# A hybrid decoder step on one core: three attention stages joined into one program, and weight casts moved from ScalarE to GpSimd

## What is computed

```
xn = rmsnorm(x) ; h = xn @ w_in                # 1024 -> fq fk fv ff fz | hq hf hi hz | mq mz | ga gb gm
A  = forgetting attention over fq, fk, fv      # 8 heads x 64, causal, plus sums of log gates
B  = gated linear recurrence (HGRN2)           # 4 heads, state 128x128, chunked
M  = attention into 256 memory tokens          # 4 heads x 128, keys and values mk, mv from mem @ w_mk, w_mv
y  = rmsnorm(x + (sig(ga)*(A*silu(fz))@w_pa + sig(gb)*(norm(B)*silu(hz))@w_pb + sig(gm)*(M*silu(mz))@w_pm) @ w_o)
```

## Time and profile before

| | us |
|---|---|
| median of 3 runs (3035.96 to 3053.45) | 3039.75 |
| the profiled execution | 3042.43 |
| its span, first to last instruction | 3040.4 |
| TensorE busy in the span | 2802.5 (92%) |
| VectorE busy | 1577.6 (52%) |
| ScalarE busy | 1098.7 (36%) |
| GpSimd busy | 728.0 (24%) |
| mean granted TensorE clock | 0.967 |

### The profile page before, as it was taken

The page is one execution under the profiler, slowest core; times in us unless marked ns, Lnnn a source line. Parts: engine busy times, 40 slices in busy tenths (PEclk is TensorE's granted clock), DMA queues, the critical chain, the costliest instruction groups (busy, mean ns, idle before and its releaser), DMA issues. The chain is left out here.

```text
span 3040.4 us, 38617 instructions
## 1 busy us (share of the span) xinstructions
PE 2802.5 (92%) x13880; PEld 2295.6 (76%) x13880; DVE 1577.6 (52%) x3007; ACT 1098.7 (36%) x2086; POOL 728.0 (24%) x743
## 2 busy tenths in 40 slices
PE   7889988899998889898789998999999978999998
PEld 5668767677776778687678877888888866888887
DVE  5414578433341467665345555656664546444544
ACT  1212111333332345443245554555554223232322
POOL 6027655123223343433020061011020014000000
PEclk9999989899998999999999999999999989999999
DMA  5576678756653656565745564555444546333331
GB/s 167 222 237 202 210 222 262 239 155 186 194 166 129 217 198 232 188 213 183 234 140 163 160 187 140 163 158 154 142 140 130 198 174 194 124 110 115 116 109 49
DMA packets 290765, 526.33 MB, mean 173 GB/s; under 512 B 110270, under 2 KB 135423, under 8 KB 269327
## 3 DMA queue, kind: packets, MB, share of 16 engines
q1 hardware_dynamic: 237519, 403.41, 42.2%
q0 software_dynamic: 17440, 55.98, 6.5%
q10 hardware_dynamic: 35616, 64.47, 5.6%
HBM read 411.09 MB, written 112.68 MB: 172 GB/s over the span
## 5 line engine op out<-in xcount | busy, mean ns | idle before, releaser
L2528 PE MATMUL fill_out<-keep_hi,fill_x 128*128 128x512 f32 x2112 | 739.8, 413 | 87.4 <-DMA fill_x<-x_tiles 47.2
L2528 PEld LDWEIGHTS fill_out<-keep_hi,fill_x 128*128 128x128 f32 x2112 | 391.7, 193 | 160.8 <-issue 36.1
L2528 PE MATMUL fill_out<-keep_lo,fill_x 128*128 128x512 f32 x1056 | 433.8, 411 | 3.9 <-PEq L3215 3.9
L413 ACT ACTIVATE fox_pt_hi<-fox_turned 128x512 fp32r<-128x512 f32 (+1 forms) x320 | 170.1, 531 | 321.2 <-PE fox_turned L363 319.3
L466 DVE TENSOR_TENSOR fox_pt_lo<-fox_turned,fox_pt_hi 128x512 fp32r<-128x512 f32 (+1 forms) x320 | 194.9, 609 | 169.2 <-ACT fox_pt_hi L413 166.7
L452 DVE CUSTOM_DVE_ANT_0 fox_probs<-fox_scores,fox_bias 128x512 f32<-128x512 f32 (+2 forms) x320 | 187.6, 609 | 106.1 <-PE fox_scores L352 56.2
L2528 PEld LDWEIGHTS fill_out<-keep_lo,fill_x 128*128 128x128 f32 x1056 | 203.6, 193 | 35.7 <-issue 4.3
L2150 ACT ACTIVATE in_stage<-in_out 128x512 f32<-128x512 f32 (+1 forms) x119 | 70.4, 594 | 433.8 <-PE in_out L99 385.2
L2628 POOL CAST keep_hi<-fill_raw 128x512 fp32r<-128x512 f32 x48 | 30.2, 628 | 652.3 <-PE fill_out L2539 616.9
L363 PE MATMUL fox_turned<-ident,fox_probs 128*128 128x128 f32 x1088 | 173.2, 274 | 7.1 <-ACT fox_probs L404 6.4
L97 PE MATMUL mf_out<-mf_w_hi,mf_t_hi 128*128 128x512 f32 x408 | 166.7, 409 | 9.0 <-DVE mf_w_lo L3031 8.1
(11 more groups left out here) (382 smaller groups left out, 6391.2 us busy)
## 6 DMA issues: line engine op xcount, KB each, us to landing
fill_x<-x_tiles SPq DMA_DIRECT2D x132, 1024.0 KB, 5.4
dc_slot<-in_cache_fox_k_dram SPq DMA_DIRECT2D x128, 256.0 KB, 3.9
dc_slot<-in_cache_fox_v_dram SPq DMA_DIRECT2D x128, 256.0 KB, 3.3
in_raw<-in_w_in_dram POOLq DMA_DIRECT2D x104, 256.0 KB, 3.6
plain<-fill_stage ACTq DMA_DIRECT2D x96, 256.0 KB, 5.5
mf_gate<-plain SPq DMA_DIRECT2D x96, 256.0 KB
turned<-in_stage ACTq DMA_DIRECT2D x64, 256.0 KB, 3.9
fill_raw<-in_w_in_dram POOLq DMA_DIRECT2D x56, 256.0 KB, 3.2
```

The source lines that it names most:

```text
L413: act.activation(pt_hi[:, zeta % PT_SLOTS, skip:BANK], bank_of(st)[:, skip:BANK], ACT.Copy).then_inc(hi_ready, 1)
L2528: ins = pe.matmul(self.out[n % self.OUTS][:], x, w, start=(k == 0 and term == 0), stop=(ends and term == 2))
```

## The change

The three stages become one Block in one `cleanup_on_exit`; what stood at a stage's start is issued near the end of the one before, and waits stand where one stage's tiles lie over another's. The recurrence's tail of 4 slots is gone; of its 96 fill matmuls 16 go to the prompt attention's first slots (two of 24, four of 12, four of 16) and 80 to its key slots. ScalarE's casts go to GpSimd in project_and_decode and in the recurrence. In the first seven passes slice k is split k ticks into the pass. The diff, without changes of indentation and cut to its core:

```diff
-    steps = [("fill", 0)] + [("queries", 0, b) for b in range(QUADS)] + [("values", 0, b) for b in range(QUADS)]
+    steps = [("open", 0), ("fill", 0), ("open", 1), ("fill", 1), ("open", 2)] + [("queries", 0, b) for b in range(QUADS)]
     for b in range(QUADS):
-        steps += [("fill", 1 + b), ("keys", 0, b)]
+        steps += [("keys", 0, b), ("fill", 2 + b)]
+    steps += [("values", 0, b) for b in range(QUADS)]
...
+                    if st == ("open", 0):
+                        recur.computed(sp)
+                        fill.wait_stored(sp, needed)
+                        load_queries(sp, 0)
+                        for n in range(2):
+                            load_keys(sp, *quads[n])
+                    if st == ("open", 1):
+                        recur.store_state(sp)
+                        recur.store_rows(sp, 0)
+                        load_values(sp, 0)
+                        load_bias(sp, 0)
+                    if st == ("open", 2):
+                        recur.store_rows(sp, 1)
+                        for n in range(2):
+                            load_z(sp, *quads[n])
...
+        split_at = steps.index(("key", *quads[-1], QUADS))
...
+        def _(sp):
+            sync_steps(sp, steps[:split_at])
...
                     if kind == "keys":
+                        if n == 0:
+                            recur.computed(pe)
...
+                    if (h, i) == (0, 0):
+                        recur.all_stored(act)
                         act.wait_ge(most_ready, h * NT + i + 1)
...
                         if i == 0:
                             dve.wait_ge(bias_loaded, 16 * (h + 1))
+                    if (h, i) == (0, 0):
+                        recur.all_stored(dve)
...
+        def computed(eng):
+            eng.wait_ge(state_ready, len(chunks))
+            eng.wait_ge(o_taken, len(chunks))
...
-        fill.begin(fill.spread(matmuls, 2 * (len(chunks) + AHEAD)) + fill.spread(last_matmuls, TAIL), True)
+        fill.begin(fill.spread(matmuls, 2 * (len(chunks) + AHEAD)))
...
+            prompt.scores_done(sp)
+            fill.wait_stored(sp, needed)
+            sp.dma_start(k_rows[:], mem_k.rearrange("(t p) c -> p t c", p=P)).then_inc(kv_loaded, 16)
+            sp.dma_start(v[:], mem_v.rearrange("(t p) c -> p t c", p=P)).then_inc(kv_loaded, 16)
+            load_q(sp, 0)
+            load_z(sp, 0)
+            load_q(sp, 1)
+            paged.sync_start(sp)
+            prompt.sync_rest(sp)
...
+            prompt.all_stored(sp)
+            load_z(sp, 1)
...
                 fill.tensor(pe, 0)
+                prompt.banks_free(pe)
                 pe.wait_ge(kv_loaded, 32)
...
-            return (n - 1) * U + (k // 2 if n < G else k)
+            return (n - 1) * U + k
...
-                def low(m):
+                def split_slice(m):
                     hi, lo = w_ring.at(ring_at[m])
+                    pool.wait_ge(raw_loaded[m % RAWS], 16 * ((m - KT) // RAWS + 1))
+                    ring_free(pool, m)
+                    pool.tensor_copy(hi, raw[m % RAWS][:]).then_inc(cast, 1)
                     pool.wait_ge(cast, m - KT + 1)
                     pool.tensor_tensor(lo, raw[m % RAWS][:], hi.bitcast(F32), ALU.subtract).then_inc(split, 1)
...
-                def high(m):
-                    act.wait_ge(raw_loaded[m % RAWS], 16 * ((m - KT) // RAWS + 1))
-                    ring_free(act, m)
-                    act.activation(w_ring.at(ring_at[m])[0], raw[m % RAWS][:], ACT.Copy).then_inc(cast, 1)
...
-MATMULS = {"recur": 1340, "recur_last": 96, "fox_first": 144, "fox": 1472, "fox_last": [10, 12], "memory_first": 16}
+MATMULS = {"recur": 1340, "fox_first": [24, 24] + [12] * 4 + [16] * 4, "fox": 1552, "fox_last": [10, 12], "memory_first": 16}
...
-                with nc.cleanup_on_exit():
-                    recur_prompt(nc, core, turned[PT["hq"]], turned[PT["hf"]], plain[PN["hi"]][0:T, :],
+                with nc.cleanup_on_exit(), nc.Block() as block:
+                    recur = recur_prompt(nc, core, block, turned[PT["hq"]], turned[PT["hf"]], plain[PN["hi"]][0:T, :],
```

More of the change, by code:

```diff
@@ L4 @@
+from collections import namedtuple
 from contextlib import ExitStack
@@ L99, in product, with attend_prompt @@
     return pe.matmul(out, a[0], b[1], start=False, stop=last)
-def attend_prompt(nc, core, queries, fox_k, fox_v, z_fox, neg_c, gated, fill, matmuls, first_matmuls, last_matmuls):
+def attend_prompt(nc, core, block, queries, fox_k, fox_v, z_fox, neg_c, gated, fill, matmuls, first_matmuls, last_matmuls, recur, needed):
     QUADS = NT // 4
@@ L488, in recur_prompt, with rows, load_queries @@
-def recur_prompt(nc, core, queries, gates, values, z_hg, gain, gated, state_out, fill, matmuls, last_matmuls, needed):
+        def rows(dram, head, first, count):
+            return dram[first * P:(first + count) * P, head * FD:(head + 1) * FD].rearrange("(t p) c -> p t c", p=P)
+        def load_queries(sp, head):
+            if head >= 1:
+                sp.wait_ge(q_ready, head * QUADS)
+            for half in range(2):
+                sp.dma_start(q_raw[half * FD:(half + 1) * FD, :],
+                             rows_of(queries, head * FD, FD)).then_inc(q_loaded, 16)
@@ new lines, in load_values, with load_keys @@
+        def load_values(sp, head):
+            if head >= 1:
+                sp.wait_ge(v_ready, head * QUADS)
+            sp.dma_start(v_raw[:], rows(fox_v, head, 0, NT)).then_inc(v_loaded, 16)
+        def load_keys(sp, head, b):
+            n = head * QUADS + b
+            if n >= 2:
+                last = quads[n - 2]
+                sp.wait_ge(turned_ready, turn_at["keys", last[0], last[1]] + 1)
+            for half in range(2):
+                sp.dma_start(k_raw[n % 2][:, :, half * FD:(half + 1) * FD], rows(fox_k, head, 4 * b, 4)
+                             ).then_inc(k_loaded[n % 2], 16)
@@ L490, in recur_prompt @@
+        return AttentionEnd(lambda sp: sync_steps(sp, steps[split_at:]), scores_done, banks_free, all_stored)
+def recur_prompt(nc, core, block, queries, gates, values, z_hg, gain, gated, state_out, fill, matmuls):
     CH = 4
@@ L502, in recur_prompt, with walk @@
     BLOCK = HH * CH
-    PARTS, AHEAD, TAIL = 4, 5, 4
-    def walk(prepare, early, late, post, extra, tail):
+    PARTS, AHEAD = 4, 5
+    def walk(prepare, early, late, post, extra):
         for n in range(-AHEAD, len(chunks)):
@@ L897, in attend_memory @@
+        return RecurrenceEnd(computed, store_state, lambda sp, piece: store(sp, BLOCKS - 1, piece), all_stored)
+def attend_memory(nc, core, block, queries, mem_k, mem_v, z_mem, gated, last, fill, first_matmuls, needed, prompt):
     ST = NM // P
```

1332 lines of the change are left out of this document (644 added, 688 removed).

## The result

The changed kernel took 3025.45 us (median of five runs, 3020.97 to 3035.83), the kernel before 3041.46 beside it: a ratio of 0.9944, 95% interval 0.9925 to 0.9964. A second set of runs gave 3022.94 against 3044.99, ratio 0.9930 (0.9909 to 0.9952). So the change takes 16 to 22 us, 0.6 to 0.7%. I had predicted 3031, 8 us less than before. The run profiled here is the slowest of its five, 3035.83 (span 3034.1); the profile of the second set has 3020.5.

The account below looks back on a forecast made before the run. TensorE, busy 2802.5 of 3040.4 us, was taken as the bound, with at most 238 us of waiting to remove. 3042.43 - 8 - 8 + 5 + 3 = 3034.4 profiled, 3031.7 against the median, stated as 3031; range 3000 to 3048.

Parts of the forecast that it names:

- First joint: Recurrence to prompt attention: overhead of about 20 us falls to 12, so -8 us (-14 to -2).
- second joint: Joint to the memory attention: 8.1 us of TensorE idle and some lowered clock go, for -8 us (-11 to -3).
- The new wait: First joint: TensorE waits for a late x tile and an eviction behind ScalarE's root, 4.5 to 9.7 us, taken as 7.
- first score about 30 us after: Sign of being right: first score about 30 us after the last recurrence matmul, with 96 fill matmuls between.
- Casts in the recurrence: Moving casts to GpSimd there only renames TensorE's wait to `keep_lo`; idle time stays and +5 us come.
- The rival that ScalarE was the cause: Recurrence: ScalarE's evictions are the real limit and GpSimd's chain keeps up, giving about 2998 us; chance 0.18.
- Casts in project_and_decode: 104 casts moved to GpSimd there cost small waits at weight changes in the later passes: +3 us, from -10 to +15.
- one slice per tick in place of two evens the first passes out: First passes of project_and_decode: splitting one slice per tick evens out GpSimd's added cast work; no gain was priced.
- VectorE beside GpSimd: Project_and_decode: GpSimd's time can become VectorE's; 24 casts would at worst put 15 us on VectorE, where 3 is taken.
- the rival at 3057: GpSimd blocks VectorE in passes 1 to 7 of project_and_decode, costing 23 us, and the recurrence's 5 doubles; chance 0.11.
- Joints that close fully: Both joints: the first's x tile comes by 1459 and no clock falls, -20 and -9, giving 3019 us; chance 0.14.
- joints that don't: Both joints: SP's earlier loads delay the x tiles as long, only -2 and -3, giving 3043 us; chance 0.09.

Follow-up runs that it names:

- e1: Changed kernel with both cast moves undone (ScalarE casts, slices split as before), joined stages kept; 3030.62 us against 3044.31 for the kernel before.
- e8: Changed kernel with ScalarE casting everywhere, slice k still split k ticks into the first seven passes; 3027.20 us against 3044.50 for the kernel before.
- e2: Kernel before with the cast moves and the spread splits alone, three stages and barriers kept; 3039.76 us against 3044.31 for the kernel before.
- e4: Changed kernel with the x tile issued ahead of the prompt attention's queries and keys at the first joint; 3019.89 us against 3044.31 before.
- e6: Changed kernel with ScalarE casting again in the last seven passes of project_and_decode; 3016.29 us against 3044.99 for the kernel before.

## Why the prediction came out right, and which of its steps did not

The time was inside the range, and the chance for no change that can be told (0.47) stood just above that for faster (0.41), which is what came: 16 and 22 us, just past the 15 that I took as the least that can be told. The joints were worked out rightly. The casts were not, and the total came near partly by luck: two terms missed on the fast side (19 and 4.6 us) stand against two too small on the slow side (11 us together).

- **First joint, -8, and second joint, -8: right.** Column E of the pairs that differ in the joints alone gives -17 (e1 against before; e8, with the same joints, gives -11) and -15 to -18 (changed against e2). By place, in the first profiles: from the last recurrence matmul to the first score 63.0 became 37.6, of which 18.2 us (80 matmuls) only moved to the key slots, so **-7**. From the last `fox_turned` to the first `mem_turned` 11.7 became 8.5, and from there to the merge 135.6 became 130.1: **-9**. The new wait was forecast at 4.5 to 9.7, taken as 7: it is 6.54 and 6.55, and its two limits, SP's queue and ScalarE's root, both show in e4. The overhead is 13 for the 12 forecast. The sign "first score about 30 us after" was not that sum: 96 fill matmuls, 16 transposes and 12 us are 36, and 37.6 came. The x tile that I had late by up to 2.4 us behind the memory loads is late by 2.29.
- **Casts in the recurrence, +5: right in kind, short in size.** The waits changed name, at the places named and for the reasons named (the differences ahead of a slice, the two raw buffers). D says +9 over all profiles. I had also misread the list: the 18.0 us for low parts are of the whole span, and 6.8 of them, in four waits, are in the recurrence. The rival that ScalarE was the cause falls: it wanted a recurrence 20 us shorter, and the recurrence is longer.
- **Casts in project_and_decode, +3: wrong, and the reason why the sum came out too small.** The step that failed is "one slice per tick in place of two evens the first passes out", which I priced at nothing, with -10 as the bound. It is -19 (A). I had read ScalarE's wait for raw loads as the only thing the move could free. I had not read GpSimd's own list, where 60.6 us for ScalarE's casts stood in the first seven passes, some 37 of them ScalarE's order and not the ring, with the cache multiplies of the decoding rows behind it. That these waits are the cause is the likeliest reading of the four cells, and no run isolates it. Against that I had also missed a cost: the sample rows use all eight slices at a pass's start, and slice 7, split in the last tick behind the multiplies, is late by 1.3 to 7.5 us in five passes.
- **The last seven passes: the working was right at one change and wrong at five.** At the last change of weights I wrote 1.2 us, from a chain of 10.6 us against a margin of 9.4; it is 1.09:

```profile
924.36 0.50 PE L98 MATMUL in_out<-rest_hi,x_first 128*128 128x512 f32 x1 [1.09 <-POOL rest_lo L2110]
```

  For the five earlier ones I took 0.3 us each, trusting decode matmuls between. They are 1.25 to 1.93 us, six in all 9.0; B says +10, and e6 takes it back.
- **The stage's end, -4.6: not in the prediction at all.** It is TensorE's wait for the recurrence's first x tile, 14.8 us before and 10.1 after. See the last section.
- **VectorE beside GpSimd**: the rival at 3057 wanted TensorE's waits for VectorE up by 15 us and the first passes longer. From 152 to 575 us these waits fell from 42 us to 24 and 23, and the passes are shorter. VectorE's busy time over column A (the same 222 instructions), before and in the two changed profiles (us, PE, PEld, DVE, ACT, POOL, clock, DMA share, GB/s):

```profile
152.16:581.68 429.52, 381.45 (x1649) 300.36 (x1649) 230.50 (x222) 83.14 (x146) 226.58 (x168) 0.94 0.73 230
153.17:570.32 417.15, 374.55 (x1649) 295.82 (x1650) 227.92 (x222) 57.29 (x99) 283.83 (x228) 0.95 0.75 240
153.53:560.69 407.16, 375.25 (x1649) 295.99 (x1649) 220.40 (x222) 57.06 (x98) 286.40 (x228) 0.95 0.77 245
```

  It falls by 3 and 10 us while GpSimd's rises by 57 and 60. The Trainium skill's rule (Advanced Engine Details and Errata, VectorE Performance Modes) is that GpSimd instructions and VectorE's two-port ones block each other at the shared port; my prediction left out the two ports. No view shows which of its instructions were two-port ones. The added casts did not make VectorE busier here.
- **Joints that close fully, joints that don't, ScalarE as the cause**: the first is refused by the 8.9 us of waits still there, the second by E, the third by D.

By the runs, the sum of the step sizes is -16 (joints) + 9 (D) - 19 (A) + 10 (B) - 4.6 (C), about -21 for a change measured at -16 and -22. The forecast's -8 lacked A and C, and had half of D and a third of B. The step sizes are means over profiles, so that the sum agrees with the totals to a few us is all that it can show.

Left open: why column A scatters by 14 us for the same code. Between the two changed profiles the 10 us are waits of TensorE (45.4 us for 34.8, the largest part at slices split late, 18.2 for 9.3), and they are there already when GpSimd ends its last multiply (377 for 367 us). No run was made for it.

## What to carry to other kernels

Moving an operation between engines is priced from the lists of all three parties: what the old engine waited for, what the new one has queued at the moment of use, and what the new engine itself stood waiting for before. The last goes with the largest term here, and it is read from the waits of an engine that is only a quarter busy. Take off it what the new engine would have to wait for all the same, as the ring's place here. A total near zero can be four effects of 5 to 20 us: measure by stage, then keep the cast where it pays (GpSimd in the first passes) and take it back where it does not (the last passes, the recurrence). And where a joint between stages closes, two or three limits wait in line behind it; moving one load forward moved the wait to the next tile.

## What the runs showed of the hardware that I had not expected

A barrier after a stage took longer when GpSimd had worked to the end. Where ScalarE cast the last eight slices, GpSimd's last difference ended at 962.49, 1.6 us before TensorE's last matmul ended, and its first instruction of the next stage came 12.04 us later:

```profile
959.92 2.57 POOL L2076 TENSOR_TENSOR keep_lo<-in_raw,keep_hi 128x512 fp32r<-128x512 f32 x2 [4.13 <-ACT keep_hi L2161]
...
974.08 1.28 ACT L721 ACT_TABLE_LOAD   x1 [9.32 <-PEq L3196]
...
974.53 1.09 POOL L2611 DMA_DIRECT2D fill_raw<-in_w_in_dram  x2 [12.04 <-POOLq L3196]
```

Where GpSimd cast them itself, its last difference ended 16 us before TensorE's last matmul:

```profile
968.69 1.28 ACT L746 ACT_TABLE_LOAD   x1 [4.64 <-PEq L3225]
...
969.13 1.09 POOL L2634 DMA_DIRECT2D fill_raw<-in_w_in_dram  x2 [21.85 <-POOLq L3225]
```

ScalarE's idle time at the barrier is 9.32 us in the one case and 4.64 in the other; from the last eviction to the first fill matmul it is 14.7 in all three profiles of the first kind and 10.1 to 10.3 in all eleven of the second. In the three, ScalarE's first instruction comes 11.6 us after the end of GpSimd's last; in the eleven it comes 5.3 us after TensorE's last matmul, whenever GpSimd was done. The last store is not the reason: it lands 3.4 us after TensorE's last matmul in both kinds. That GpSimd arrives at a barrier some 6 to 10 us after its last instruction (an estimate from these numbers) would explain both, but no run took that apart. Also unexpected was how long SP can sit on one issue: at the first joint, with 0.93 of the DMA engines' time in use, the bias row took 6.53 us to issue, and the x tile stood behind it. It took 3.9 to 6.8 us in all twelve profiles with joined stages, and 0.50 in the two without.
